# A norm's scaled tile feeds the rounded copy and the remainder directly, and GpSimd writes the biased tile

## The reference, cut to what matters

```
x <- LN1(ALPHA*x + mix(x) @ w_out)
x <- LN2(ALPHA*x + conv_gated_ffn(x))

def layernorm(x, g, b):
    mu = mean(x); xc = x - mu; var = mean(xc * xc)
    return xc * rsqrt(var + 1e-5) * g + b
```

## Time and profile before

| | us |
|---|---|
| median of 3 runs | 2431.37 |
| lowest and highest | 2425.22, 2433.13 |
| the profiled execution, as timed | 2434.02 |
| span of its profile | 2432.2 |
| PE busy | 2296.1 (94%) |
| DVE busy | 1188.9 (49%) |
| ACT busy | 825.8 (34%) |
| POOL busy | 120.1 (5%) |

### The profile page before, as it was taken

One profiled execution on the slowest core, in us unless ns is written; L12 is line 12 of the kernel. 1 busy time (PEld: TensorE's weight loads), 2 busy tenths in 40 slices (PEclk: granted clock), 3 DMA queues, 4 the chain that ended last, 5 costly groups with the idle time before them and its releaser, 6 DMA issues.

```text
span 2432.2 us, 43416 instructions
## 1 busy us (share of the span) xinstructions
PE 2296.1 (94%) x17556; PEld 2084.0 (86%) x17556; DVE 1188.9 (49%) x1902; ACT 825.8 (34%) x1478; POOL 120.1 (5%) x132
## 2 busy tenths in 40 slices
PE   8989998999997999999889899989999979999996
PEld 7966666799996999999788666667999969999996
DVE  3744443534346664565347444434333466636654
ACT  3333343423314341332243343334233153313322
POOL 0012220000000000000000122200000000000000
PEclk9989998899998999999999899989999989999998
DMA  5245540022221222222123455400222212322231
GB/s 181 85 137 173 176 157 1 1 87 78 86 83 36 78 92 84 70 85 97 53 83 97 135 176 173 140 1 10 86 85 79 81 38 78 101 75 78 78 102 44
DMA packets 57104, 217.48 MB, mean 89 GB/s; under 512 B 7280, under 2 KB 8176, under 8 KB 56880
## 3 DMA queue, kind: packets, MB, share of 16 engines
q1 hardware_dynamic: 34128, 132.29, 17.1%
q0 software_dynamic: 18432, 75.51, 9.5%
q10 hardware_dynamic: 4448, 8.33, 1.0%
HBM read 211.19 MB, written 4.90 MB: 89 GB/s over the span
## 4 chain that ended last, share of the span: by engine, by line
PE 91%; DVE 4%; ACT 3%; DMA 1%; DVEq 1%; issue 1%; ACTq 0%; SPq 0%
PE PS L698 61%; PE PS L856 5%; PE PS L880 5%; PE PS L900 4%; PE PS L869 2%; PE PS L729 2%; PE PS L1009 1%; PE PS L886 1%; PE PS L718 1%; PE PS L987 1%; ACT m_X L409 1%; PE PS L998 1%; ACT m_XH L382 1%; DVE m_RN L1090 1%; PE PS L939 1%; PE PS L984 1%
## 5 line engine op out<-in xcount | busy, mean ns | idle before, releaser
L698 PE MATMUL PS<-m_XH,m_WH 128*128 128x288 f32 x2560 | 730.0, 299 | 50.8 <-DVE m_XL L1068 38.0
L698 PE MATMUL PS<-m_XL,m_WH 128*128 128x288 f32 x2560 | 721.9, 297 | 0.0
L698 PE MATMUL PS<-m_XH,m_WL 128*128 128x288 f32 x2560 | 553.5, 298 | 0.0
L698 PEld LDWEIGHTS PS<-m_XH,m_WH 128*128 128x128 f32 x2560 | 486.1, 190 | 57.5 <-issue 34.3
L698 PEld LDWEIGHTS PS<-m_XL,m_WH 128*128 128x128 f32 x2560 | 487.2, 190 | 0.5
L698 PEld LDWEIGHTS PS<-m_XH,m_WL 128*128 128x128 f32 x2560 | 414.2, 190 | 0.0
L1068 DVE TENSOR_TENSOR m_WL<-m_WS,m_WH 128x1024 fp32r<-128x1024 f32 (+2 forms) x228 | 292.1, 1281 | 224.1 <-ACT m_WH L382 213.2
L382 ACT ACTIVATE m_WH<-m_WS 128x1024 fp32r<-128x1024 f32 (+2 forms) x228 | 251.8, 1104 | 410.3 <-PE PS L698 403.1
L698 PE MATMUL PS<-m_HH,m_WH 128*128 128x288 f32 x704 | 198.9, 296 | 0.0
L698 PE MATMUL PS<-m_HL,m_WH 128*128 128x288 f32 x704 | 197.6, 295 | 0.0
L369 POOL DMA_INDIRECT m_RAW<-in_cache_rows,m_IDXS x128 | 119.9, 937 | 1443.3 <-DVE m_YC L1265 977.0
(11 more groups left out here) (266 smaller groups left out, 3030.5 us busy)
## 6 DMA issues: line engine op xcount, KB each, us to landing
m_WS<-in_w_units SPq DMA_DIRECT2D x192, 512.0 KB
m_WS<-in_w_units SPq DMA_DIRECT2D x32, 704.0 KB
m_X<-in_x_t SPq DMA_DIRECT2D x4, 576.0 KB, 9.0
m_WS<-in_w_units SPq DMA_DIRECT2D x4, 576.0 KB
out_y<-m_X SPq DMA_DIRECT2D x4, 576.0 KB, 2.8
m_RAW<-in_cache_rows,m_IDXS POOLq DMA_INDIRECT x128, 5.3
m_BRI<-in_branch_in ACTq DMA_DIRECT2D x2, 760.0 KB, 4.9
m_CST<-in_consts SPq DMA_DIRECT2D x1, 1426.5 KB, 13.4
```

What stands on the lines that cost most here:

```text
L698: mm = pe.matmul(PS[0:rows, 2 * par + h, (1 - h) * at0:(1 - h) * at0 + HT], w(part, k), x(k)[:, h * HT:(h + 1) * HT], start=(k == 0 and pa ...
```

## The change

- DVE's multiply of a norm becomes a `scalar_tensor_tensor` that applies the gain (a value per partition from `PAR`) and `RN` together.
- ACT writes `XH` straight from the scaled tile with the bias added (`Identity` with a bias alone); its in-place instruction for gain and bias is gone, except in the norm n = 3, where it stays with the bias alone.
- DVE's split reads the scaled tile, adds the bias and subtracts `XH` in one `scalar_tensor_tensor`.
- POOL adds the bias to `X` in place, tile by tile, after the split of that tile, for n = 0, 1 and 2 (`n_x` now counts these).
- Three waits on `n_x` are new: DVE before it overwrites `PAR` in layer 1, ACT before the mixing stage's copy of `X` in layer 1, and DVE before the residual of the FFN.

```diff
--- before.py
+++ after.py
@@ -374,6 +374,11 @@
                 for n in range(RAWS):
                     pool.wait_ge(S[f"g_landed{n}"], 32 * landings(l, n, NU2))
                 past(pool)
+                for n, b0 in ((2 * l, C_1B), (2 * l + 1, C_2B))[0:2 if l < DEPTH - 1 else 1]:
+                    for k in range(DT):
+                        pool.wait_ge(S["n_lo"], (n + 1) * DT + k + 1)
+                        pool.tensor_scalar(X[:, k, :], X[:, k, :], PAR[:, b0 + k:b0 + k + 1], None, ALU.add)\
+                            .then_inc(S["n_x"], 1)
 
 
         @block.scalar
@@ -397,7 +402,7 @@
                 if k in (1, 3):
                     weight_hi(k // 2, k // 2)
 
-            def norm(n, g0, b0):
+            def norm(n, b0):
 
                 for k in range(DT):
                     act.wait_ge(S["n_xc"], n * DT + k + 1)
@@ -406,11 +411,11 @@
                 nc.scalar.activation(RN[:, :], RN[:, :], ACT.Sqrt).then_inc(S["n_std"], 1)
                 for k in range(DT):
                     act.wait_ge(S["n_xn"], n * DT + k + 1)
-                    nc.scalar.activation(X[:, k, :], X[:, k, :], ACT.Identity, bias=PAR[:, b0 + k:b0 + k + 1],
-                                         scale=PAR[:, g0 + k:g0 + k + 1]).then_inc(S["n_x"], 1)
+                    bias = PAR[:, b0 + k:b0 + k + 1]
                     if n < 2 * DEPTH - 1:
-                        act.wait_ge(S["n_x"], n * DT + k + 1)
-                        copy(XH[:, k, :], X[:, k, :]).then_inc(S["n_hi"], 1)
+                        nc.scalar.activation(XH[:, k, :], X[:, k, :], ACT.Identity, bias=bias).then_inc(S["n_hi"], 1)
+                    else:
+                        nc.scalar.activation(X[:, k, :], X[:, k, :], ACT.Identity, bias=bias).then_inc(S["n_x"], 1)
 
             for l in range(DEPTH):
 
@@ -616,6 +621,8 @@
                 meet(act, "met_act", l, 2)
 
 
+                if l > 0:
+                    act.wait_ge(S["n_x"], 2 * l * DT)
                 for k in range(DT):
                     copy(XH[:, k, :], X[:, k, :]).then_inc(S["xr_hi"], 1)
                 copy(YH[:, 0:2, :], YA[:, :, :])
@@ -637,7 +644,7 @@
                 for m in range(DT):
                     act.wait_ge(S[f"mm_done{m % 2}"], CREDIT[f"mm_done{m % 2}"] + l * NM + M_OUT + m // 2 + 1)
                     weight_hi(l * NU + U_OUT + m + 2, m % 2)
-                norm(2 * l, C_1G, C_1B)
+                norm(2 * l, C_1B)
 
 
                 act.wait_ge(S["sf_in"], (l + 1) * 16)
@@ -675,7 +682,7 @@
                             act.wait_ge(S[f"mm_done{m % 2}"], CREDIT[f"mm_done{m % 2}"] + l * NM + M_FFN + M_HALF * hf + FH + m // 2 + 1)
                             weight_hi(u, m % 2, UW if m < DT - 2 else D)
                     act.wait_ge(S["stored"], (l * N_STORES + 6 + hf) * 16)
-                norm(2 * l + 1, C_2G, C_2B)
+                norm(2 * l + 1, C_2B)
 
 
         @block.tensor
@@ -1074,9 +1081,13 @@
 
             def norm(n):
 
+                g0, b0 = (C_1G, C_1B) if n % 2 == 0 else (C_2G, C_2B)
+
                 def split(k):
                     dve.wait_ge(S["n_hi"], n * DT + k + 1)
-                    lo(XL[:, k, :], X[:, k, :], XH[:, k, :]).then_inc(S["n_lo"], 1)
+                    dve.scalar_tensor_tensor(out=XL[:, k, :], in0=X[:, k, :], scalar=PAR[:, b0 + k:b0 + k + 1],
+                                             in1=XH[:, k, :].bitcast(F32), op0=ALU.add, op1=ALU.subtract)\
+                        .then_inc(S["n_lo"], 1)
 
                 dve.wait_ge(S["n_sum"], n + 1)
                 for k in range(DT):
@@ -1091,7 +1102,8 @@
                 dve.drain()
                 last = n == 2 * DEPTH - 1
                 for k in range(DT):
-                    dve.tensor_tensor(X[:, k, :], X[:, k, :], RN[:, :], ALU.mult).then_inc(S["n_xn"], 1)
+                    dve.scalar_tensor_tensor(out=X[:, k, :], in0=X[:, k, :], scalar=PAR[:, g0 + k:g0 + k + 1],
+                                             in1=RN[:, :], op0=ALU.mult, op1=ALU.mult).then_inc(S["n_xn"], 1)
                     if k >= 2 and not last:
                         split(k - 2)
                 if not last:
@@ -1120,6 +1132,8 @@
             dve.tensor_copy(IDXS[:, :, :], PTF[:, :, :])
             dve.wait_ge(S["params"], 16)
             for l in range(DEPTH):
+                if l > 0:
+                    dve.wait_ge(S["n_x"], 2 * l * DT)
                 dve.tensor_copy(PAR[:, :], PARS[:, bass.ds(l, 1), :].rearrange("p o n -> p (o n)"))\
                     .then_inc(S["par_set"], 1)
                 dve.memset(EX[:, :, 0:KEEP], 0.0)
@@ -1513,6 +1527,8 @@
                     up_tile(hf, FH - 1, UW)
                     dve.memset(XS[:, :], 0.0)
                     dve.drain()
+                    dve.wait_ge(S["n_x"], (2 * l + 1) * DT)
+                    past(dve)
                     for m in range(DT):
                         par = m % 2
                         dve.wait_ge(S[f"mm_done{par}"], CREDIT[f"mm_done{par}"] + l * NM + M_FFN + M_HALF * hf + FH + m // 2 + 1)
```

## The result

The changed kernel takes 2440.02 us (median of 6 runs, 2434.15 to 2447.77), against 2429.16 for the kernel before in the same rounds (6 runs, 2425.22 to 2433.13). The ratio is 1.0045, 95% interval 1.0025 to 1.0065: slower by 0.45%. The forecast was 2428.0, a gain of 3.4 us; the direction was wrong. The measured time lies within the stated range, in the part above 2430 that the range had for its first rival. The profiled execution took 2440.73 around a span of 2438.9, 6.7 longer than the span before.

The account below looks back on a forecast made before the run. PE, busy 94% of the span, was taken as the bound, with ACT pacing the norms. Gains of 3.1 (norms 0 and 2), 0 (norm 1) and 0.2 (norm 3) sum to 3.4 us: 2428.0 from the median 2431.37; range up to 2444.

Parts of the forecast that it names:

- first rival: DVE in the norms: POOL's SBUF reads block DVE's two-input instructions; +14.6 us at T = 1.0, +6.4 at 0.59; chance 0.28.
- The pace of DVE: DVE's multiplies and splits in a norm: 16 instructions at 0.73 us from start to start.
- the last split at 11.8: DVE's split 7 ends 11.8 us after a norm's first multiply, where it ended at 13.5 before.
- the gain in norms 0 and 2: PE's first tile ends at 12.9 instead of 14.46: 1.6 us in each norm, together 3.1.
- the small gain of norm 3: End of the kernel: ACT's last instruction ends at 2428.7 instead of 2428.96, a gain of 0.2 us.
- POOL's price: Each POOL bias addition in norms 0 to 2 was taken as 1.0 us, between bounds of 0.59 and 3.75.
- the term of norm 1: DVE's parameter copy waits for POOL and starts at 13.4 as before: 0 us; 1.0 gained with POOL at 0.59.
- What moves that copy moves PE one for one.: Norm 1: any shift of DVE's parameter copy shifts PE's third tile, behind the branch inputs' DMA, by the same time.
- DVE at 0.85: Rival: waits cost DVE's overlap in the norms, so DVE becomes the bound; last split at 13.6, net +0.9 us; chance 0.12.
- POOL's reads hold DVE up: Rival in the norms: six POOL additions each delay DVE by their full time T, split 7 ending at 11.8 + 6T; chance 0.28.
- POOL being late: Rival: POOL's additions delay norm 1's parameter copy, by clash or plain slowness; net +3.0 us at T = 1.0; chance 0.13.
- a POOL that is kept out: Form of the late-POOL rival: DVE wins the clash, POOL's eight additions start after split 7, norm 1's copy 6.4 us late.

## Why the prediction was wrong

**What held.** The pace of DVE, 0.73, with no loss at the waits, wherever POOL is quiet; ACT's 0.77; the last split at 11.8 and the gain in norms 0 and 2; the small gain of norm 3 (first multiply to end of span 10.2 before, 9.95 after, the 0.2 of the forecast). The kernel without POOL's additions shows them together: 4.1 below the kernel before (1.2 to 7.3), the size of the forecast.

**The first step that failed: POOL's price.** "I take 1.0: ACT's 855 for this shape plus POOL's own shortest, 118, which is also close to its 937." It is 1.73 alone and 1.95 beside a busy DVE. The value was between the bounds, 0.59 and 3.75, but it was taken from ACT and from a gather's issue, neither of which is POOL's elementwise work. The step behind it was right: above about 1.24 "the copy starts at 3.05 + 8T", which with 1.95 to 2.0 gives 18.7 to 19.1; measured 19.1. So the term of norm 1, priced at 0, was 5.7 at the copy. The kernel with doubled additions confirms the dependence. In the one without the wait the copy comes at 14.2 and the third tile 4.5 earlier.
The Trainium skill, GPSIMD Engine Reference, section 3.1, led to an estimate of 0.87 for 576 columns; this case measures 1.73 with a per-partition operand, twice that.

**The second: the pace of DVE beside POOL.** The forecast let "16 instructions at 0.73" run on while POOL adds. Five of them took 1.22 to 1.30 instead of 0.81, and the 3.1 of norms 0 and 2 became a loss of 2.3. Without POOL, and with POOL started after the last split, all sixteen keep 0.73.

**A smaller one: "What moves that copy moves PE one for one."** The DMA behind the copy does not always take the same: 5.71 before, 5.32 without POOL's additions, 4.3 to 4.4 in the kernels where it was issued later. So 5.7 at the copy were 4.4 at the tile, and 1.6 with half of the columns were 0.3. Why it takes less I did not test. One of the sums slips as well: with DVE at 0.85 POOL's last three additions of 1.0 would begin at 11.9 and end at 14.9, 1.5 late and not 1.2.

**The rival that was half right.** "POOL's reads hold DVE up" had 0.28 and is what happened, at a smaller price. It took six instructions each holding DVE for all of T; five were met, and each held it for 0.41 to 0.49. The stretch goes with POOL's columns (0.25 for half of them), does not depend on the tile, and is absent with POOL's short memsets. It costs 2.4 at the last split, which turns the gain of 1.6 in norms 0 and 2 into a loss of 0.7 at PE's second tile (its start is 15.15 after the first multiply, 14.46 before). POOL then works on for 5 us beyond the norm, over the first instructions of the FFN; at the third tap the loss is 1.1. This second part the rival did not have. POOL being late, which had 0.13, came true beside it, as plain slowness and not as a POOL that is kept out: it started at 761.93, in the middle of the norm.
The Trainium skill, SBUF — State Buffer, section Who interferes with whom, says that such a DVE instruction contends with a POOL instruction that reads SBUF and not with one that only writes. The additions show the first; the memsets agree with the second, as far as they reach. The Trainium skill's Terms on that page say that the ports the two engines share are held for the full instruction and that the loser fully blocks; here DVE lost at most 0.49 to a POOL instruction of 1.95, so that part is measured otherwise.

**Not foreseen.** In norm 1 a wait of PE that grew from 0.98 to 4.54 brought PE down to its lower clock, 1.8 more. The clock fell in the same wait of two other kernels: with POOL on the spare tile PE stood for 5.8 and the tile's 48 matmuls took 7.93, and with doubled additions it stood for 18.9 and they took 9.21. In the other kernels PE stood there for under 2 us, and the clock stayed at 1.00. Against it, the DMA of the branch inputs took 1.35 less when issued later.

**The sum, in the prediction's terms.** Norms 0 and 2: 1.1 lost in each instead of 3.1 gained in both. Norm 1: 5.7 - 1.35 + 1.8 = 6.2 lost instead of 0. Norm 3: 0.2 gained. Together +8.2, against 10.9 measured with an interval of about 6 to 16. The prediction would have given slower with POOL at 2.0 and DVE undisturbed only by 5.6 - 3.4 = 2.2 us; the stretch, the clock and POOL's work over the FFN are the rest.

What stays open: PE's pace between the norms, 6.32 or 6.45 for the same 48 matmuls, differs between executions and between the norms of one. The long stretches scatter more than the terms above: from PE's fourth tile of layer 1 to norm 2, which the changes hardly touch, the ten profiled executions took between 716.5 (doubled additions) and 724.5 (spare tile). I didn't look for the cause. So the terms are to be read from the rows within a norm, and a single execution's time proves none of them. Nor did I test the fall of the clock by itself; its 1.8 is read from the rows. Whether POOL's writes ever hold DVE is open as well.

## What to carry to other kernels

An engine that is 5% busy is not free: price its instruction by a row of that very engine and kind, and where there is none, let the wait that hangs on it decide how far the range goes. Ask of work given to POOL what it reads while DVE runs, and who waits for the last of it; if DVE is the pace of the stretch, ACT's gaps are the better place, and here they held all of it at no cost that the times show. A wait put in front of an instruction that seems small (a copy of parameters) delays all that is queued behind it, here three DMAs and the weights of the next layer.

## What the runs showed of the hardware

- A POOL `tensor_scalar` with a per-partition operand on 128 x 576 float32: 1.73 beside an idle DVE, 1.95 beside a busy one (1.78 on the spare tile), 2.87 for the first of a norm; on 128 x 288 about 0.98 (3.47 for three, less 1.51, halved), and 1.51 beside a busy DVE. A memset of 128 x 576: 0.58.
- Such a POOL instruction holds a DVE instruction with two SBUF inputs for 0.41 to 0.49 when it has 576 columns, about 0.25 when it has 288. DVE instructions with one SBUF input are hit as hard: a copy of 128 x 2 became 0.64 from 0.16, a `tensor_scalar` of 128 x 592 became 1.08 from 0.59. Not every one that overlaps is hit (0.59 in the first FFN row above).
- After an idle stretch of 8.5 to 8.7 us in a norm PE restarts at a granted clock of 0.50. It is back at 1.00 some 3 us later in about half of the 30 norms profiled (norms 0 to 2 of ten kernels), 5.5 to 6.1 in ten, and 9 to 12.7 in four. One of these is norm 0 of the kernel with the bias from the table of both layers, where it stayed at 0.50 for some 12 us with PE busy most of the time. Windows of that kernel (PE's busy time is the first after the length, PEclk the third number from the end):

```profile
756.07:760.00 3.93, 3.92 (x15) 3.57 (x16) 3.93 (x5) 1.55 (x2) 3.88 (x2) 0.50 0.00 0
760.00:764.00 4.00, 3.72 (x14) 3.03 (x14) 4.00 (x5) 1.55 (x2) 4.00 (x3) 0.50 0.00 0
764.00:768.00 4.00, 3.86 (x17) 3.51 (x16) 3.05 (x6) 2.06 (x2) 4.00 (x3) 0.50 0.00 0
768.00:772.00 4.00, 4.00 (x30) 4.00 (x30) 1.18 (x3) 1.76 (x4) 4.00 (x3) 0.90 0.02 4
```

PE's second tile began 16.3 after the first multiply here and 15.15 in the changed kernel, with the splits at the same times: 1.2 us that no change of the kernel explains. By the third tap 0.3 of it was left (30.2 against 29.9).
